# GpSimd's second weight unit behind a norm waits for VectorE's raw low parts

## What is computed

```python
def rms_norm(x, g):
    y = x * lax.rsqrt(jnp.mean(x * x, axis=-1, keepdims=True) + EPS)
    return y * g

# first block
x = x + 0.5 * swiglu(rms_norm(x, g_ffn1), w1_gate, w1_up, w1_down)    # norm 0
proj = rms_norm(x, g_mix) @ w_in                                      # norm 1
x = x + merged @ w_out                                                # two attentions, merged
x = x + 0.5 * swiglu(rms_norm(x, g_ffn2), w2_gate, w2_up, w2_down)    # norm 2
# second block
proj = rmsnorm(h, g_mix_2) @ w_in_2                                   # norm 3
h = h + merged @ w_o_2                                                # retention, delta rule, merged
up = causal_dwconv(rmsnorm(h, g_ffn_2) @ w_up_2, ffn_conv_w_2)        # norm 4
```

## Time and profile before

| | us |
|---|---|
| median of 3 runs | 2679.41 (2678.58 to 2681.46) |
| the profiled execution | 2682.5 |
| its span, first to last instruction | 2680.2 |
| TensorE busy | 2432.2 (91%) |
| VectorE busy | 1110.1 (41%) |
| ScalarE busy | 846.6 (32%) |
| GpSimd busy | 873.7 (33%) |

### The profile page before, as it was taken

How to read it: one execution, slowest core, us unless ns; L and a number is a source line. 1 busy time by engine, 2 the same in 40 slices (tenths; PEclk the granted TensorE clock), 3 DMA queues, 4 the chain that set the end, 5 groups by cost and what they waited for, 6 DMA issues and landing times.

```text
span 2680.2 us, 28210 instructions
## 1 busy us (share of the span) xinstructions
PE 2432.2 (91%) x11226; PEld 1961.5 (73%) x11226; DVE 1110.1 (41%) x1452; ACT 846.6 (32%) x825; POOL 873.7 (33%) x384
## 2 busy tenths in 40 slices
PE   7999999999999999999997995959595989999898
PEld 6888777766567788887775774849484877788786
DVE  6322025656434722105406106363636322877602
ACT  4222224375343422213234223140404122433312
POOL 3443442332124344344321333121212034344333
PEclk9999999999999999999996997989897999999998
DMA  4332231322222233223220121010101012222222
GB/s 129 95 97 83 86 118 59 79 57 58 79 83 87 94 96 104 70 93 106 82 63 32 48 95 47 24 40 17 47 17 45 19 55 93 88 94 94 67 91 77
DMA packets 151312, 194.84 MB, mean 73 GB/s; under 512 B 11628, under 2 KB 104119, under 8 KB 151223
## 3 DMA queue, kind: packets, MB, share of 16 engines
q1 hardware_dynamic: 146560, 192.97, 22.7%
q10 hardware_dynamic: 4663, 0.61, 0.1%
HBM read 187.25 MB, written 6.29 MB: 72 GB/s over the span
## 4 chain that ended last, share of the span: by engine, by line
PE 67%; issue 14%; DVE 11%; ACT 4%; POOL 4%; DMA 0%; SPq 0%; POOLq 0%; DVEq 0%; ACTq 0%
PE PS L166 17%; PE PS L168 16%; PE PS L167 16%; POOL wl L157 4%; DVE cv L1915 2%; PE PS L1797 2%; PE PS L1806 2%; DVE h_lo L309 1%; PE PS L1457 1%; PE PS L1005 1%; PE PS L1805 1%; ACT wh L148 1%; PE PS L193 1%; PE PS L194 1%; PE PS L195 1%
## 5 line engine op out<-in xcount | busy, mean ns | idle before, releaser
L157 POOL TENSOR_TENSOR wl<-raw,wh 128x2048 fp32r<-128x2048 f32 (+1 forms) x214 | 806.4, 3770 | 1468.6 <-ACT wh L148 1468.5
L166 PE MATMUL PS<-h_hi,wh 128*128 128x512 f32 x1696 | 680.9, 401 | 24.9 <-DVE h_lo L309 11.5
L148 ACT ACTIVATE wh<-raw 128x2048 fp32r<-128x2048 f32 (+1 forms) x214 | 339.4, 1589 | 1045.2 <-PE PS L168 983.9
L168 PE MATMUL PS<-h_hi,wl 128*128 128x512 f32 x1696 | 667.3, 393 | 0.0
L167 PE MATMUL PS<-h_lo,wh 128*128 128x512 f32 x1696 | 667.2, 393 | 0.0
L166 PEld LDWEIGHTS PS<-h_hi,wh 128*128 128x128 f32 x1696 | 323.5, 191 | 111.6 <-issue 19.8
L168 PEld LDWEIGHTS PS<-h_hi,wl 128*128 128x128 f32 x1696 | 322.5, 190 | 69.3
L167 PEld LDWEIGHTS PS<-h_lo,wh 128*128 128x128 f32 x1696 | 323.8, 191 | 64.9 <-issue 0.7
L166 PE MATMUL PS<-act_hi,wh 128*128 (+1 forms) x528 | 210.0, 398 | 7.9 <-POOL wl L157 6.6
L167 PE MATMUL PS<-act_lo,wh 128*128 (+1 forms) x528 | 209.3, 396 | 0.0
L168 PE MATMUL PS<-act_hi,wl 128*128 (+1 forms) x528 | 209.3, 396 | 0.0
(11 more groups left out here) (440 smaller groups left out, 3269.3 us busy)
## 6 DMA issues: line engine op xcount, KB each, us to landing
raw<-in_w_in_dram SPq DMA_DIRECT2D x104, 512.0 KB, 4.7
raw<-in_w_up_dram SPq DMA_DIRECT2D x88, 512.0 KB, 4.8
raw<-in_w_down_dram SPq DMA_DIRECT2D x132, 256.0 KB, 2.8
raw<-in_w_gate_dram SPq DMA_DIRECT2D x44, 512.0 KB, 4.0
raw<-in_w_out_dram SPq DMA_DIRECT2D x16, 256.0 KB, 2.8
raw<-in_w_ret_br_dram SPq DMA_DIRECT2D x8, 512.0 KB, 4.5
raw<-in_w_dn_br_dram SPq DMA_DIRECT2D x8, 512.0 KB, 4.5
raw<-in_w_o_dram SPq DMA_DIRECT2D x16, 256.0 KB, 2.9
```

Source lines behind the costliest of these rows:

```text
L148: nc.scalar.activation(wh[:, slot, 0:size], raw[:, slot, 0:size], ACT.Copy).then_inc(w_hi, 1)
L157: nc.gpsimd.tensor_tensor(wl[:, slot, 0:size], raw[:, slot, 0:size], wh[:, slot, 0:size].bitcast(F32), ALU.subtract).then_inc(w_lo, 1)
L166: nc.tensor.matmul(dst, sh, mh, start=start, stop=False)
L168: return nc.tensor.matmul(dst, sl, mh, start=False, stop=stop)
```

## The change

GpSimd's first low part behind a norm stays as it was. Ahead of the second it waits for h_ready at 2 * KD * n + KD (KD = 8), that is, for all eight raw low parts of this norm. norm_pool gets the norm's number for it.

```diff
-    def norm_pool(pool, u):
-        los(pool, u, 2)
+    def norm_pool(pool, n, u):
+        los(pool, u, 1)
+        pool.wait_ge(h_ready, 2 * KD * n + KD)
+        los(pool, u + 1, 1)
@@
-            norm_pool(pool, U["up0"])
+            norm_pool(pool, 0, U["up0"])
...
-            norm_pool(pool, U["mid1"])
+            norm_pool(pool, 1, U["mid1"])
...
-            norm_pool(pool, U["up1"])
+            norm_pool(pool, 2, U["up1"])
...
-            norm_pool(pool, U["ret"])
+            norm_pool(pool, 3, U["ret"])
...
-            norm_pool(pool, U["up2"])
+            norm_pool(pool, 4, U["up2"])
```

## The result

The change makes the kernel slower. Over 20 runs of each the median went from 2678.16 to 2686.39 us; the ratio of the means (2678.66 and 2685.31) is 1.0025, with a 95% interval of 1.0018 to 1.0032, so +6.7 us (4.8 to 8.6). In the experiments some executions, of the kernel before as well, took 3163 us and more, and the ratios leave these out. The forecast was no change, 2678.8 us, with a range up to 2685.0. The profiled execution of the changed kernel has a span of 2685.1 us, 4.9 more than that of the kernel before. In the runs with extra matmuls or split subtractions they are higher too: there the sum's 343 and 344 can be 348 and 349, and the adds' 352 can be 357 or 362.

A forecast was written before the change was run, and what follows sets the result against it. TensorE carries two thirds of the chain, with waits behind five norms for VectorE work held by GpSimd's subtraction. Norm terms +0.4, -0.7, +0.9, -0.5, -0.7 summed to -0.6 us: 2678.8, range 2675.0 to 2685.0.

The forecast's parts named there:

- The hold and the order of the adds: Behind each norm, GpSimd's moved subtraction leaves VectorE's first add free and holds the second; norm_pe's first row 0.67 us earlier.
- Rival 1: GpSimd's subtraction gets in ahead of VectorE's first add, which ends 0.35 us later; +4.4 us, 2683.8; chance 0.15.
- rival 3: VectorE's adds are not held by the subtraction, or slip in between; each norm gives 4.3 us, 2658; chance 0.05.
- The fourth unit's load: SyncE's load goes out some 6.5 us later, landing near 2292; 13 us of cover before ScalarE's rounding, no price.
- The head of the second unit: TensorE behind the long stop: 8 matmuls at low clock cost 1.6 us in norms 0, 2, 3, 4.
- the clock's price: Low clock after TensorE's joined stop: bounds 0, 1.6 and 2.1 us; 1.6 taken, nothing new in norm 1.
- What reaches the end: Behind each norm, VectorE's line 0.67 us earlier and TensorE's 0.93 later; later TensorE waits can absorb its delay.
- the prediction's upper bound for the clock: Most that low clock behind TensorE's stop could cost, 2.1 us, taken from the 6.58 us wait ending at 2544.13.
- the later waits: TensorE's waits of 0.55 us at 82.66, 1.83 at 1295.36 and 2.08 at 2339.01 take up its delay.
- Forecast +0.4, -0.7, +0.9, -0.5, -0.7: Predicted shifts in us reaching the end from norms 0 to 4, together -0.6.
- Rival 2: The long standstill costs two stretches of low clock, 3.2 us, behind each norm's adds; +6.6 us, 2686.0; chance 0.07.

The follow-up runs named there:

- e1: The changed kernel with 20 extra matmuls between the first weight unit and norm_pe, filling TensorE's stop; ratio 0.9983 against the kernel before.
- e4: The changed kernel with the moved wait in norms 1 and 3 only; ratio 1.0008 against the kernel before.
- e5: The changed kernel with the moved wait in norms 0, 2 and 4 only; ratio 1.0008 against the kernel before.
- e8: The changed kernel with the second unit's subtraction in two halves, the second only after ScalarE's root; ratio 0.9980 against the kernel before.
- e10: The changed kernel with the subtraction halved around ScalarE's root, 11 matmuls in the stop, masks of norms 1 and 3 between halves; 0.9943 against the kernel before.

## Why the prediction was wrong

**The hold and the order of the adds: right, to 0.25 us.** The first add is free and the second is held in norm 4. By norms 0 to 4 the sum comes 0.51, 0.72, 0.64, 0.74 and 0.68 us earlier behind the first unit's start (forecast 0.67, and 0.5 in norm 3), and the stop is 4.8 to 5.2 us (5.0). One term was right without its reason. The prediction has GpSimd start at 2282.0 and end at 2287.0; with the 4.6 us that it names it would end at 2286.6. The row has the missing 0.4 us: GpSimd, started during the first add, took 4.99 us. And the first add does wait for a signal of another engine, ScalarE's sq_ready (the prediction says that it needs none); it had been given long before, as ScalarE's first squares end at 2284.77 and the add starts at 2286.20. Rival 1 (GpSimd ahead of the first add) and rival 3 (adds not held) fell with those rows. The fourth unit's load had its cover, as said: ScalarE rounds that unit at 2310.19 and waits 0.19 us, for TensorE and not for the load.

**The head of the second unit: right.** From the second unit's first matmul to the third's, norm 4, before and after:

```profile
2292.82 0.80 PE L166 MATMUL PS<-h_hi,wh 128*128 128x512 f32 x1
...
2304.13 0.39 PE L166 MATMUL PS<-h_hi,wh 128*128 128x512 f32 x1
```

```profile
2297.01 1.42 PE L166 MATMUL PS<-h_hi,wh 128*128 128x512 f32 x1
...
2309.93 0.39 PE L166 MATMUL PS<-h_hi,wh 128*128 128x512 f32 x1
```

11.31 and 12.92 us: 1.61, with 1.6 forecast. By the same count norms 0, 2 and 3 lose 1.7, 1.5 and 1.4, and norm 1 0.15, which had been low before.

**First step that failed: the sum's own matmuls were put at nothing in the clock's price.** "What reaches the end" has VectorE's line 0.67 earlier. But this line runs through norm_pe, the first thing behind the stop and so the first at 1.2 GHz. From the sum to the second unit's first matmul it takes 1.09 us instead of 0.56 in norms 0, 2 and 4 (2297.01 - 2295.92), and the root starts 2.11 us behind the sum instead of 1.16 (2298.03 - 2295.92; before 2293.42 - 2292.26). In norms 1 and 3, with the eight records of small matmuls, 2.79 instead of 1.46. In norm 4 VectorE's line is therefore -0.68 + 0.95 = 0.27 later, not 0.67 earlier, and TensorE's -0.68 + 0.53 + 1.61 = 1.46 later instead of 0.93. TensorE's line loses 0.53 + 1.61 = 2.14 us, which is the prediction's upper bound for the clock (2.1); VectorE's line, for which it had no such term, loses 0.95. The clock was priced only on the work that the argument was about, not on all that follows the stop. e1 shows it from the other side: with the stop filled, the sum's row takes 1.13 us again and these terms are gone.

**Second step that failed: the later waits don't take TensorE's delay up.** The prediction let it sink into the wait at 2339 of norm 4. That wait is as long as before, and 1.45 us later behind the first unit's start (2344.80 - 2279.99 = 64.81, before 63.36):

```profile
2344.80 0.80 PE L166 MATMUL PS<-h_hi,wh 128*128 128x512 f32 x1 [2.07 <-POOL wl L157]
```

The two lines are not apart. It begins with the fourth unit, whose rounding at 2310.19 is 0.58 us later behind the first unit's start than before (30.20 and 29.62), 0.3 us more than VectorE's line. ScalarE's rounding of the fifth unit waits for TensorE's use of the third; before it stood behind ScalarE's own work, now TensorE is the later:

```profile
2315.26 1.92 ACT L148 ACTIVATE wh<-raw 128x2048 fp32r<-128x2048 f32 x1
```

```profile
2321.07 1.92 ACT L148 ACTIVATE wh<-raw 128x2048 fp32r<-128x2048 f32 x1 [0.88 <-PE PS L168]
```

It comes 41.08 us behind the first unit's start instead of 39.61, GpSimd's subtraction with it, and that falls on four VectorE instructions of the convolution. They end 1.65 us behind it in both traces (2323.51 - 2321.86, 2329.31 - 2327.66), so they are later by as much as it is. Before and after:

```profile
2318.29 5.22 DVE L535 TENSOR_SCALAR work<-work,vecs 128x512 f32<-128x512 f32 x4
```

```profile
2323.15 6.16 DVE L537 TENSOR_SCALAR work<-work,vecs 128x512 f32<-128x512 f32 x4
```

So TensorE's 1.46 us came back on VectorE's line. Only norm 3 has the wait shorter, as forecast (0.81 us where it was 1.83), and even there VectorE's line is 1.0 later, not 0.5 earlier. That is the first term again: the sum is 0.74 us earlier, and the root starts 3.98 us behind it instead of 2.22.

```profile
1298.62 1.97 PE L1420 MATMUL PS<-ident,work 128*128 128x128 f32 x16 [0.81 <-DVE work L713]
```

(1298.62 - 1244.01 = 54.61, before 1295.36 - 1241.76 = 53.60; 1244.01 and 1241.76 are the first unit's starts of norm 3.)

The stage behind norm 4 ends only 0.56 us later all the same. Of the 1.45 us at 2344.80, 1.38 are left at the end of TensorE's wait of 6.6 us. But there more of the low clock falls into the wait and less on work, 3.1 us where it was 4.5. Before, the rows are in the earlier trace rows; after:

```profile
2549.85 0.79 PE L166 MATMUL PS<-act_hi,wh 128*128 x1 [6.57 <-POOL wl L157]
...
2552.00:2554.00 2.00, 2.00 (x8) 0.76 0.54 191
```

A window at 0.76 has 0.97 us of its 2 at the low clock, so the clock is low until 2552.97, and before until 2548.64. That gives back about 0.65 us, and another 0.2 us comes from the stretch near the end (2667 us before). Which part of a low stretch meets work isn't fixed by the change, so that stage 4's +0.56 is near the forecast's steps is luck.

**The sum.** Forecast +0.4, -0.7, +0.9, -0.5, -0.7; the traces have +0.9, +1.0, +1.35, +2.1, +0.6. With this first term put in (0.95 us on VectorE's line in norms 0, 2 and 4, 1.3 in norm 1, 1.8 in norm 3, and 0.53 on TensorE's) the forecast's own steps give +0.9, +0.7, +1.5, +1.3, +0.3, together +4.7 of the traces' +5.9. For norm 4 that agreement is the luck just told. Norm 0's is open too, since stage 0 differs by 0.7 us between two traces without the wait (e4). Of norm 3's +2.1, 1.0 is there at 1298.62. The rest arises in the long recurrent stages, first by a stretch of low clock (0.50 from 1332 to 1334) that the trace of before lacks; e1 has it too (0.50 from 1324 to 1326), so it isn't the long stop's doing. With norm 1's spread of 3 us between traces (e5) this rest can't be given to the change. Rival 2 named the right cause, the long stop's clock, and +6.6 us; that this is the measured +6.7 is luck. Its mechanism, 3.2 us lost and over 5 us of low clock behind each sum, is not what the windows show: 4.5 us of low clock behind the sum and 2.14 us lost in norm 4, on more work than was counted.

## What to carry to other kernels

A wait that is moved along one engine's line of work gains next to nothing (0.7 us of 4.3 here) unless the place it moves to is off that line; e8 to e10 put half of it beside a reciprocal, which kept its 3.35 us, and gained. When a change joins two short stops of TensorE into a long one, price every instruction behind it at the low clock, the small ones that others wait for first. Then compare the traces row by row from a common start: a stage's length alone mixes the change with stretches of low clock that fall otherwise later. A delay sinks into a later wait only if nothing that ends this wait is itself fed by the delayed engine.

## What was not expected of the hardware

With the clock low, the two records of the sum's matmul took 1132 ns each by the median, instead of 678, and the stop ahead of it was 4.8 to 5.2 us. A stop's length alone doesn't tell: in e8 the clock was low at the sum after 2.6 us in norms 1, 2 and 4, and at 1.00 in norm 0 after 2.61. A GpSimd subtraction of 2048 columns that starts during a VectorE add takes 4.99 us instead of 4.56; the add keeps its 0.68.
